# Memory attention and the index projection in one loop: eight steps with a unit of the one and an eighth of the other, in single PSUM banks

## What is computed

```python
h = rmsnorm(x, g_mix)
proj = h @ w_in            # q_s k_s v_s | q_d k_d v_d | q_i k_i w_i | q_m | gates
o_swa = sliding_window_attention(rope(q_s), rope(k_s), v_s, sinks)   # 8 heads, window 128
o_dsa = dsa_attention(rope(q_d), rope(k_d), v_d, rope(q_i), rope(k_i), w_i * scale)
o_mem = memory_cross_attention(q_m, mem_k, mem_v)                     # 4 heads, 256 keys
```

## Time and profile before

| | us |
|---|---|
| median of 3 runs (2639.22 to 2640.80) | 2640.07 |
| the profiled execution | 2647.66 |
| its span | 2645.9 |
| PE busy (matmul) | 2482.5 |
| DVE busy | 1588.8 |
| ACT busy | 1203.2 |
| POOL busy | 834.6 |

### The profile page before, as it was taken

How to read it: one execution, slowest core, us unless ns; L and a number is a source line. 1 busy time by engine, 2 the same in 40 slices (tenths; PEclk the granted TensorE clock), 3 DMA queues, 4 the chain that set the end, 5 groups by cost and what they waited for, 6 DMA issues and landing times. The chain is left out here.

```text
span 2645.9 us, 32798 instructions
## 1 busy us (share of the span) xinstructions
PE 2482.5 (94%) x11852; PEld 2023.9 (76%) x11852; DVE 1588.8 (60%) x2820; ACT 1203.2 (45%) x2222; POOL 834.6 (32%) x748
## 2 busy tenths in 40 slices
PE   4997899999899999999999999999898999999997
PEld 3765688887677778887888887778776888878886
DVE  5347458988555687765545776334758444356666
ACT  6136346745511455554333453225526555443343
POOL 0222332221220066663252400005303565514242
PEclk9999899999999999999999999999999999999998
DMA  4102122323263256657754455424242444396354
GB/s 160 47 13 83 35 62 91 97 96 113 97 200 104 80 180 214 198 195 267 255 178 143 153 175 182 77 72 135 73 175 100 157 150 152 133 344 191 132 163 150
DMA packets 191187, 371.91 MB, mean 141 GB/s; under 512 B 13724, under 2 KB 58404, under 8 KB 190772
## 3 DMA queue, kind: packets, MB, share of 16 engines
q1 hardware_dynamic: 178676, 342.56, 39.2%
q10 hardware_dynamic: 8064, 14.68, 1.5%
q0 software_dynamic: 4288, 12.60, 1.5%
HBM read 269.05 MB, written 100.74 MB: 140 GB/s over the span
## 5 line engine op out<-in xcount | busy, mean ns | idle before, releaser
L2797 PE MATMUL bank<-hq_hi,wq_hi 128*128 128x512 f32 x896 | 352.7, 394 | 18.2 <-DVE hq_lo L1938 8.6
L2824 PE MATMUL bank<-ring_b_hi,ring_a_hi 128*128 128x512 f32 x896 | 350.7, 391 | 6.3 <-DVE hidden L1982 5.2
L2798 PE MATMUL bank<-hq_lo,wq_hi 128*128 128x512 f32 x896 | 350.6, 391 | 0.0
L2799 PE MATMUL bank<-hq_hi,wq_lo 128*128 128x512 f32 x896 | 350.5, 391 | 0.0
L2826 PE MATMUL bank<-ring_b_hi,ring_a_lo 128*128 128x512 f32 x896 | 350.1, 391 | 0.0
L2825 PE MATMUL bank<-ring_b_lo,ring_a_hi 128*128 128x512 f32 x896 | 350.1, 391 | 0.0
L2141 DVE TENSOR_TENSOR ring_a_lo<-a_raw,ring_a_hi 128x1024 fp32r<-128x1024 f32 x112 | 153.1, 1367 | 227.5 <-ACT ring_a_hi L1337 227.3
L1337 ACT ACTIVATE ring_a_hi<-a_raw 128x1024 fp32r<-128x1024 f32 x112 | 118.7, 1060 | 336.3 <-PE bank L2826 331.0
L1927 DVE TENSOR_TENSOR wq_lo<-unit_raw,wq_hi 128x512 fp32r<-128x512 f32 x160 | 164.4, 1030 | 108.9 <-ACT wq_hi L1185 106.0
L2797 PEld LDWEIGHTS bank<-hq_hi,wq_hi 128*128 128x128 f32 x896 | 169.4, 189 | 56.6 <-DVE hq_lo L1938 14.6
L2824 PEld LDWEIGHTS bank<-ring_b_hi,ring_a_hi 128*128 128x128 f32 x896 | 169.2, 189 | 42.7 <-DVE hidden L1982 6.1
(11 more groups left out here) (466 smaller groups left out, 5532.9 us busy)
## 6 DMA issues: line engine op xcount, KB each, us to landing
a_raw<-hidden_scratch SPq DMA_DIRECT2D x112, 512.0 KB, 3.3
hidden_scratch<-hidden SPq DMA_DIRECT2D x32, 1024.0 KB, 4.8
w_raw<-in_w_in SPq DMA_DIRECT2D x104, 256.0 KB, 2.8
hidden_scratch<-hidden SPq DMA_DIRECT2D x32, 768.0 KB, 3.6
unit_raw<-in_w_mlp_in SPq DMA_DIRECT2D x16, 1024.0 KB, 5.7
b_raw<-in_w_mlp_out SPq DMA_DIRECT2D x32, 512.0 KB, 4.4
unit_raw<-in_w_ff SPq DMA_DIRECT2D x16, 1024.0 KB, 5.4
b_raw<-in_w_ff SPq DMA_DIRECT2D x32, 512.0 KB, 4.7
```

Of the source, the lines that this page charges most:

```text
L2797: mm(o, lh[:, q, :], rh[:, q, :], start=(fresh and q == 0), stop=False, skip_group_check=True)
L2798: mm(o, lh[:, q, :], rl[:, q, :], start=False, stop=False, skip_group_check=True)
L2799: l = mm(o, ll[:, q, :], rh[:, q, :], start=False, stop=(q == 3), skip_group_check=True)
L2824: mm(o, ra_hi[r][:, e, js], rb_hi[r][:, e, :], start=(fresh and v == 0 and e == 0), stop=False, skip_group_check=True)
```

## The change

Both stages become one loop of eight steps (v = 0 to 7) with a tail. Step v of PE: scores of unit v+1, half of the projection of block v (12 matmuls), transposes of unit v, the other half, output of unit v-1, rope transposes of block v-1. So that both fit in eight banks, each use has a single bank: scores 0 and 1, outputs 2, the projection 3, rope transposes 4 and 5, probability transposes 6 and 7. Buffers that overlapped are laid apart; some go into the low half of `W[1]`, free once the memory queries are made, and POOL copies the memory keys and values there. C_IDX is split during the sliding window attention, one piece in every odd unit. C_GATE's pieces are split at the loop's end. The wait for the stores is split in two: for those of the window attention in step 0, for the rest ahead of C_GATE's last piece.

```diff
+        LO1 = 3 * CH
+        k_mem = at("k_mem", [P, 2, MEM], f32, LO1)
+        v_mem = at("v_mem", [P, 2, MEM], f32, LO1 + 10240)
...
+        def out_bank(u):
+            return 2 if u >= NSWA else 2 + u % 2
...
                 if r == 16:
-                    for u in range(NSWA + 8):
+                    for u in range(NSWA - 2):
                         store(u)
+                    pool.wait_ge(qm_mm, 4)
+                    nc.gpsimd.tensor_copy(k_mem[:, :, :], k_mT[:, :, :]).then_inc(mem_kept.sem, 1)
+                    nc.gpsimd.tensor_copy(v_mem[:, :, :], v_m[:, :, :]).then_inc(mem_kept.sem, 1)
+                    for u in range(NSWA - 2, NSWA):
+                        store(u)
+                elif r >= 18:
+                    store(r - 2)
...
+                    if u % 2 and u < u1:
+                        split_hi(C_IDX, 0, 20, [u // 2])
...
             attend(0, NSWA)
-            split_hi(C_IDX, 0, 20)
-            attend(NSWA, NSWA + 8)
-            for r in range(16, 24):
-                rope_evac(r, 3, r % 8)
-                split_hi(C_GATE, 1, None, [r - 16])
+            att_exp(NSWA)
+            for v in range(10):
+                u = NSWA + v
+                if v >= 2:
+                    rope_evac(14 + v, 3, v - 2)
+                if v < 7:
+                    att_exp(u + 1)
+                if v < 8:
+                    att_pt(u)
+                if 1 <= v < 9:
+                    att_oh(u - 1)
+                if v >= 7:
+                    split_hi(C_GATE, 1, None, range(2 * v - 14, 2 * v - 12))
+            split_hi(C_GATE, 1, None, range(6, 8))
...
+                    if u % 2 and u < u1:
+                        split_lo(C_IDX, 0, [u // 2])
...
+            att_scores(NSWA)
+            for v in range(10):
+                u = NSWA + v
+                if v < 8:
+                    att_norm(u)
+                if v < 7:
+                    att_scores(u + 1)
+                if v >= 2:
+                    att_lo(u - 2)
+                    index_lo(v - 2)
+                if v == 0:
+                    for b in range(2):
+                        dve.wait_ge(at_od[b], 16 * NSWA)
+                if v < 8:
+                    rope_products(16 + v, 20 + v, 3, v)
+                else:
+                    split_lo(C_GATE, 1, range(3 * v - 24, 3 * v - 21))
+            split_lo(C_GATE, 1, (6,))
             for b in range(2):
                 dve.wait_ge(at_od[b], 16 * (NSWA + 8))
...
+            split_lo(C_GATE, 1, (7,))
...
             def rope_transposes(r, kind, need):
                 pe.wait_ge(*need)
-                if r >= 2:
+                if kind == 3:
+                    pe.wait_ge(r_ev, r)
+                    pe.wait_ge(r_lo, r - 16)
+                elif r >= 2:
                     pe.wait_ge(r_ev, r - 1)
...
-                if kind == "swa" and u:
+                if u:
                     pe.wait_ge(at_s, u)
-                elif kind == "mem":
-                    pe.wait_ge(at_s, u - 1)
...
                 pe.wait_ge(at_pt, u + 1)
-                if u >= 2:
+                if u >= NSWA:
+                    pe.wait_ge(at_ol, u)
+                elif u >= 2:
                     pe.wait_ge(at_ol, u - 1)
...
-            attend(NSWA, NSWA + 8)
+
+            def index_part(t, k0, k1):
+
+                g = 20 + t
+                if k0 == 0:
+                    pe.wait_ge(group_free, g)
+                for k in range(k0, k1):
+                    lh, ll = tok(hT, k, t)
+                    rh, rl = W[0][0][:, k, 0:452], W[0][1][:, k, 0:452]
+                    mm(bank[3][:, 0:452], lh, rh, start=(k == 0), stop=False)
+                    mm(bank[3][:, 0:452], lh, rl, start=False, stop=False)
+                    l = mm(bank[3][:, 0:452], ll, rh, start=False, stop=(k == 7))
+                if k1 == 8:
+                    l.then_inc(group_done, 1)
+
+            chunk_ready(C_IDX)
+            pe.wait_ge(mem_kept.sem, mem_kept.base + 2)
+            att_scores(NSWA)
+            for v in range(9):
+                u = NSWA + v
+                if v < 7:
+                    att_scores(u + 1)
+                if v < 8:
+                    index_part(v, 0, 4)
+                    att_transposes(u)
+                    index_part(v, 4, 8)
+                if v:
+                    att_out(u - 1)
+                    rope_transposes(15 + v, 3, (r_q, 16 + v))
             pe.wait_ge(at_ol, NSWA + 8)
...
-            chunk_ready(C_IDX)
-            for r in range(16, 26):
-                if r < 24:
-                    natural(C_IDX, 0, 4 + r, r % 8, 452)
-                else:
-                    gate_steps(0, 2 * (r - 24), 2 * (r - 24) + 2)
-                if r >= 18:
-                    rope_transposes(r - 2, 3, (r_q, r - 1))
-
+            gate_steps(0, 0, 4)
```

More of the change, by code:

```diff
@@ L135, in build @@
         kd = [at(f"rope_k{i}", [P, 256], f32, t3 + 7168 * i + 6144) for i in range(2)]
+        for j, (n, o) in enumerate(zip("abq", (ra, rb, qr))):
+            o += [at(f"rope_index_{n}{i}", [P, 512], f32, s2 + 12288 + 6144 * i + 2048 * j) for i in range(2)]
+        LO1 = 3 * CH
+        k_mem = at("k_mem", [P, 2, MEM], f32, LO1)
+        v_mem = at("v_mem", [P, 2, MEM], f32, LO1 + 10240)
+        kd += [at(f"rope_index_k{i}", [P, 256], f32, LO1 + 12288 + 1024 * i) for i in range(2)]
         pr = at("probs", [P, 3, 4, 256], f32, t3)
@@ L139, in build @@
         ol = [at("attn_lo0", [P, 256], f32r, t3 + 13312), at("attn_lo1", [P, 256], f32r, s3 + 9216)]
+        pt += [at(f"mem_probsT{i}", [P, 2, 512], f32, LO1 + 2048 + 4096 * i) for i in range(2)]
+        oh += [oh[0], at("mem_attn_hi1", [P, 256], f32r, LO1 + 14336)]
+        ol += [ol[0], at("mem_attn_lo1", [P, 256], f32r, LO1 + 15360)]
         memx = at("memx", [P, 2, D], f32, s3 + 10240)
@@ L771, in _ @@
                     rotate(r, Q2, 2, 4, 0, True).then_inc(r_q, 1)
+            for u in range(NSWA + 6, NSWA + 8):
+                store(u)
             def split_lo(c, par):
@@ L1034, in att_oh @@
                     act.wait_ge(at_od[u % 2], 32 * (u // 2))
-                A_(oh[u % 2][:, :], bank[2 + u % 2][:, 0:256], ACT.Copy).then_inc(at_oh, 1)
+                A_(oh[unit_slot(u)][:, :], bank[out_bank(u)][:, 0:256], ACT.Copy).then_inc(at_oh, 1)
             def attend(u0, u1):
@@ L1596, in rope_products @@
                     dve.wait_ge(r_q, r - 1)
-                ps = bank[g % 4]
+                ps = bank[3 if kind == 3 else g % 4]
                 if kind == 1:
@@ L1672, in index_lo @@
                 dve.wait_ge(r_ev, 17 + t)
-                tt(k_iT[1][:, ts], XB[t % 2][:, P:2 * P], k_iT[0][:, ts].bitcast(f32), ALU.subtract)
+                tt(k_iT[1][:, ts], XB[0][:, P:2 * P], k_iT[0][:, ts].bitcast(f32), ALU.subtract)
                 for h in range(4):
                     q = q_iT[h][64:128, ts]
-                    l = tt(q, XB[2 + t % 2][64:128, h * P:(h + 1) * P], q.bitcast(f32), ALU.subtract)
+                    l = tt(q, XB[1][64:128, h * P:(h + 1) * P], q.bitcast(f32), ALU.subtract)
                 l.then_inc(r_lo, 1)
[L1679 to L1686, removed]
+            att_scores(NSWA)
[16 more added lines that the diff above has]
+            split_lo(C_GATE, 1, (6,))
+            for b in range(2):
+                dve.wait_ge(at_od[b], 16 * (NSWA + 8))
+            split_lo(C_GATE, 1, (7,))
             dve.wait_ge(r_tr, 24)
@@ L2505, in att_scores @@
                     else:
-                        l_, r_ = q_mT[hs, 4 * c + b // 2, (b % 2) * P:(b % 2 + 1) * P], k_mT[hs, c, :]
-                    l = mm((bank if kind == "swa" or u % 2 else XB)[par][:, (i // 2) * nk:(i // 2 + 1) * nk], l_, r_, start=True, stop=True)
+                        l_, r_ = q_mT[hs, 4 * c + b // 2, (b % 2) * P:(b % 2 + 1) * P], k_mem[hs, c, :]
+                    l = mm(bank[par][:, (i // 2) * nk:(i // 2 + 1) * nk], l_, r_, start=True, stop=True)
                 l.then_inc(at_sc, 1)
```

51 lines of the change are left out of this document (26 added, 25 removed).

## The result

| | before | changed |
|---|---|---|
| median of 4 runs, us | 2640.44 | 2656.12 |
| lowest to highest | 2639.22 to 2641.18 | 2654.47 to 2664.34 |
| profiled execution, span | 2645.9 | 2662.5 |

The ratio is 1.0056 (95% interval 1.004 to 1.0073): the change costs 15.7 us. The forecast was 21.3 us saved. It was wrong in sign, and yet the loop that the change is named after does what was forecast. The loss is in a stage that the loop doesn't touch.

What follows compares the result with a forecast made beforehand. PE was taken to bound what follows a hole in the memory stage: 26.4 - 0.7 - 1.2 - 2.2 - 1.0 = 21.3 us saved, from a median of 2640.07 to 2618.8 us; range 2612 to 2631.

Steps and rivals of the forecast that it cites:

- What bounds it, and where the saving was to come from: PE bounds what follows a hole of some 20 us in the memory stage; third index-score unit 26.4 us earlier.
- The step: One step of the merged loop is set by PE at 9.2 us, with nothing waiting.
- The tail: Behind the loop's steps, a chain through ACT and DVE of 6.0 us, gates 2.8, first relu at 338.3.
- deductions for hops and clock: In the merged loop, shape changes and semaphore hops 0.15 us a step, 1.2 in all; half clock at its start 2.2.
- (c) the copies: POOL's two copies of 128x512 ahead of the loop: nothing taken; PE 3 us late if each cost 4 us.
- (d) the stores' wait: DVE's new wait for the window attention's stores: they land before DVE reaches it, so it costs nothing.
- (a) C_IDX in the window attention: Splitting C_IDX during window attention costs 0.1 us for each of eight, 0.7 with rounding, between 0 and 4.8.
- (e) the clock: PE at half clock for the loop's first three pieces, 2.2 us taken of 4.3; 1 more in the tail.
- 1, single banks: In the merged loop each bank handover adds 0.2 to 0.3 us; step 10.4, 8 us lost, 2627; chance 0.14.
- 2, ports: In the loop POOL's rotation and DVE exclude each other on shared ports; 16 us lost, 2635; chance 0.06.
- 3, the clock in the loop: Short waits keep PE at 1.2 GHz, 7.6 us more a step; with four slow steps 2649; chance 0.06.
- 4: No net effect: work behind the loop doesn't start earlier, held by stores or weights; 2639; chance 0.05.

Runs made afterwards that it cites:

- run 3: The changed kernel, but DVE takes the C_IDX piece whose high part ACT made two units ago; 2622.56 us, ratio 0.9923 to the kernel before.
- run 2: The changed kernel, but DVE makes the low part of each C_IDX piece one unit later; 2628.80 us, ratio 0.9945 to the kernel before.
- 8: run 2 with another tail: ACT makes four C_GATE high parts at step 7's start, DVE spreads pieces 0 to 3 over steps 7 to 9; 2623.08 us.

## Why the prediction was wrong, point by point

- **What bounds it, and where the saving was to come from: right.** The stretch from the first memory scores to the third unit of index scores went from 115.4 to 91.4 us. Forecast: 26.4 less 1.2, 2.2 and 1.0, that is 22.0; measured 24.0. It stayed saved to the end. (Two of the sums are a little off: step 0 adds up to 10.3, not 10.4, and the third unit comes at 339.9, not 340.1. Neither matters.)
- **The step: right.** 9.39 us (340.16 to 349.55) for 9.2 + 0.15, at clock 1.00, and the engines beside PE had 6.2, 4.65 and 5.1 us for the forecast 6.1, 4.6 and 5.3. In the window's row (columns as in the earlier trace rows) no engine but PE is near the step.

```profile
340.16:349.55 9.39, 9.39 (x64) 7.93 (x63) 6.21 (x26) 4.65 (x18) 5.10 (x14) 1.00 0.09 28
```

- **The tail: the sum right, in part by luck.** The first relu came 90.2 us after the first memory scores. The forecast had 87.2, and 90.6 with its deductions for hops and clock (1.2 and 2.2). Its chain left out a wait: C_GATE's own piece 4 must be reloaded too. From the low part of piece 0 (371.6) to the high part of piece 4 (376.16) it took 4.6 us, where the earlier trace rows gave 3.05, and DVE stood 1.73 us for it; the next chunk's reload, the one in the forecast, took 2.8 (377.5 to 380.27). Against that, PE reached the gate products 81.9 us after the first memory scores, for 83.6 in the forecast with deductions. The two cancel in the relu.

```profile
370.89 1.90 DVE L1576 TENSOR_TENSOR w_lo<-w_raw,w_hi 128x512 fp32r<-128x512 f32 x3
376.16 1.92 ACT L985 ACTIVATE w_hi<-w_raw 128x512 fp32r<-128x512 f32 x3 [3.15 <-DMA w_raw<-in_w_in]
376.83 1.98 DVE L1576 TENSOR_TENSOR w_lo<-w_raw,w_hi 128x512 fp32r<-128x512 f32 x3 [1.73 <-ACT w_hi L985]
380.27 1.41 ACT L985 ACTIVATE w_hi<-w_raw 128x512 fp32r<-128x512 f32 x2 [0.83 <-DMA w_raw<-in_w_in]
381.59 0.85 ACT L1139 ACTIVATE bank<-bank 128x384 f32<-128x384 f32 x2
```

- **(c) the copies: right,** 0.6 us apiece, hidden; **(d) the stores' wait: right.**

```profile
284.55 0.62 POOL L777 COPY k_mem<-k_mT 128x512 f32<-128x512 f32 x1
285.11 0.61 POOL L778 COPY v_mem<-v_m 128x512 f32<-128x512 f32 x1
```

- **(a) C_IDX in the window attention: this step failed.** It said that the high part "falls into ACT's 1.20 us of idle time and the low part (0.6) into DVE's 0.75, neither on that chain", 0.7 us in all and 4.8 at most. It cost 40.2. I had fitted each piece into its own engine's idle time, and had not asked when the high part is ready for DVE: the added wait (`w_hi`) was not costed at all, nor what is queued behind it on DVE (`att_scores(u+1)`) and who waits for that (PE). The idle time was there, at the wrong moment of the unit. Even the upper bound was a sum of work, and the price of a wait isn't bounded by work. The work itself was sized rightly: with the wait gone (run 3) a pair takes 9.37 us for 9.36, and the kernel saves 19.7 us of the 21.3 forecast.
- **(e) the clock:** scores 16 ran at full clock, 17 and part of the first projection at half (mean 0.91 in 291 to 309). It cost 1.1 us, half of the 2.2 taken: the third scores started 11.33 us after the first, for 10.19 in run 2 at full clock. But the clock was most expensive where I had not looked for it, behind the eight waits.
- **Rivals.** 1, single banks: no; no handover in steps 2 to 6 made PE wait (the profile has no wait of PE between 309 and 364). 2, ports: no; the rotation took 3.7 us in the loop (1.97 + 1.71), less than the 4 to 5 forecast, and POOL's 5.1 us fitted. 3, the clock in the loop: it stood at 1.00, with one bank for each use. By the Trainium skill's rule that I had set against the change (TensorE: Matmul & The Clock Gate, "A second HAM failure mode: psum-queue depth-cycling") the loop would have paid; it did not, but the rule names PE's short idles as the cause, and the loop's profile shows none (busy 50.0 of 50.0 us), so this is no test of it. The row that I gave in its favour was misread: in a memory unit, with 1.48 us idle, the clock was 1.00, and the mean of 0.77 comes from 256 to 270 and from 295 to 305 (0.50). 4: no. The sign turned for a reason that none of the five names, and the 7% for slower stood for another one.

```profile
340.30 1.97 POOL L756 TENSOR_TENSOR rope_index_k<-rope_index_a,rope_index_b 128x32 f32<-128x32 f32 x8 [3.40 <-DVE rope_index_b L1645]
342.24 1.71 POOL L756 TENSOR_TENSOR rope_index_q<-rope_index_a,rope_index_b 128x128 f32<-128x128 f32 x4
```

## What to carry to other kernels

When work of two engines is put into their idle time and one part feeds the other, write down for the consumer when the producer's queue reaches it, and what stands behind the consumer. If the producer stands behind an instruction that waits for a third engine, and that engine waits for what is queued behind the consumer, the two pieces close a loop, however small they are. The remedy was free here (run 3): let the consumer take the piece of the round before, and look at whether "a round later" is also later in time.

## What the runs showed of the hardware that I had not expected

- **A short wait costs more than itself.** A piece's wait, 3.24 us on PE in most cases, cost 5.0 us (40.2 in eight; two pieces at once 5.8, 23.3 in four), since the granted clock fell to half behind it: matmuls of 512 columns at 0.42 instead of 0.23 us apart. The Trainium skill (TensorE: Matmul & The Clock Gate, "HAM oscillation — how this bites in real kernels") says that a loop whose waits let the clock fall pays for it in each turn; the trace agrees, mean clock 0.86 in 180 to 240 against 1.00.
- **The clock moves the marks from run to run.** Runs 2 and 8 have the same code up to the first memory scores and reach them at 249.98 and 253.97: at half clock for longer around 170 us (means of 0.72 and 0.60 in 170 to 180) and again at the stage's end (1.00 and 0.81 in 240 to 250). Run 3's kernel reached the mark at 250.97 in one profile and at 253.66 in the other. Up to four microseconds of this mark are not the edit's.
- **POOL's rotation is longer beside a low part of weights.** In the kernel before, six of the eight rotations have DVE's C_GATE low part (0.69 us) beside their four large combinations, which take 2.18 to 2.22 us; in the other two, and in all eight of the loop, which has no such low part beside them, they take 1.69 to 1.71 us. So the 2.21 of the earlier trace rows goes with that one instruction and not with DVE's work at large. No run varies this alone, and the cause is not shown.
